# Memory norm's products spread on DVE, and four final products given to POOL and ACT, in a decoder layer on eight cores

## The chip, the cores and the metric

The kernel runs on one Trainium2 chip, on all 8 cores. Each core computes one of the eight batch entries, with no exchange between cores. The metric is the device time in microseconds of the slowest core, as the median of several runs. A profile is one execution, read on the slowest of its cores.

## The reference, cut to what matters

The layer is a SwiGLU half, a mixer of three branches (latent attention, gated linear attention, cross-attention into 256 memory tokens), a second SwiGLU half, and a final RMSNorm. The change touches the norm of the memory tokens and the final norm.

```python
def _rmsnorm(x, g):
    y = x * lax.rsqrt(jnp.mean(x * x, axis=-1, keepdims=True) + EPS)
    return y * g

def _swiglu(x, wg, wu, wd):
    return (jax.nn.silu(x @ wg) * (x @ wu)) @ wd

def _cross(xq, mem_n, w_kv):
    kv = (mem_n @ w_kv).reshape(B, M, 2, X_HEADS, X_DH)
    ...

h = x + 0.5 * _swiglu(_rmsnorm(x, ffn1_norm), ffn1_wg, ffn1_wu, ffn1_wd)
h = h + _mixer(h, mem, positions, ...)    # holds _cross(xq, _rmsnorm(mem, mem_norm), x_w_kv)
h = h + 0.5 * _swiglu(_rmsnorm(h, ffn2_norm), ffn2_wg, ffn2_wu, ffn2_wd)
return _rmsnorm(h, final_norm)
```

D_MODEL is 1024, D_FF 2816, and each core has 2048 tokens.

## The kernel before

**Tiles.** Activations lie with channels on the 128 partitions and tokens along the free axis. A core's 2048 tokens are four tiles of 512. The residual of a tile is eight slices of 128x512 in f32; three tiles' residuals are on the chip at once. Two of them are printed as `hS` in the rows, the third as `ntm`, because it shares that memory.

**The first channel mixer** (`ffn` with `f1_d`, the SwiGLU half) runs for tiles 0, 1 and 2 together. The 22 blocks of D_FF are cut into stages of 5, 5, 4, 4 and 4 (`SPLIT`, L443). A stage first does gate and up for each block and each of the tiles: 16 matmuls, a Silu on ACT, a product on DVE. Then it does the down products: for each of eight output slices and each tile one PSUM bank of 5 or 4 matmuls, and an evacuation on DVE, which adds it to the residual (`stt`, L599). The gate and up weights of a block are one DMA (`ring<-f1g`), the down weights of a stage of five are four DMAs (`ring<-f1d`, one for two of the eight slices); POOL's queue issues both, and they are converted from f32 to bf16 on the way. Seven ring buffers hold them (limit `rf`). POOL also issues `wb<-wm` conversions, which prepare later weights in DRAM.

**Memory keys and values** (`memory_kv`, L923) run inside the first mixer. At block 5 the memory tokens are loaded and normed: squares on ACT, a sum by matmuls with ones on PE, Ln and Exp on ACT for the reciprocal root, then eight products on DVE (`rmsnorm`, L751; `mb<-ma,vecs_s`, 128x256 each). At block 8 four weights `xw` are asked for, and 64 matmuls of 256 columns make keys and values.

**The ending** (`ending`, L1412) treats the last tile in two halves of 256 tokens. For each half come eight down products, their evacuations (128x256), squares on ACT and a sum in PSUM. Then per half `power` (L747) takes Ln and Exp, and eight products `scaled` (L811) multiply the residual slice by the final weight and the reciprocal root, in place. After the fourth and the eighth of them a DMA stores four slices.

**What sets the order.** Nothing is ordered by hand. Each operation is added with an engine and a cost, and `schedule` (L216) plays the program with these costs and writes down the order in which each engine takes them; on the chip each engine follows that order strictly. Among operations that are ready, the one with the lowest priority number goes first. The number is the operation's place in the program plus `f.base`, so a large `f.base` means: only when nothing nearer is ready. Pools of buffers are dealt in program order, ring buffers and PSUM banks by the planner. The waits are put in as semaphores, and `dma` (L205) passes through the same planner.

```python
op.pri = self.base + seq
...
pri = [op.pri for op in ops]
```

Of the kernel before, what the change touches and what calls it, by code (L numbers as in the profile page):

```python
# [13 lines left out]
D = 1024  # L14
# [443 lines left out]
def build_program():  # L458
# [185 lines left out]
    def vcol(c):  # L644
        return vecs[:, c:c + 1]
# [277 lines left out]
    def memory_kv():  # L923
        memf = [M2.get() for _ in range(4)]
        for i in range(4):
            f.dma("sp", memf[i], mem_d[i], nbytes=262144, after=f.last_pe, slack=12.0)
        src = [memf[c // 2][:, (c % 2) * 256:(c % 2 + 1) * 256] for c in range(8)]
        mt = [M1.get() for _ in range(4)]
        dst = [mt[c // 2][:, (c % 2) * 256:(c % 2 + 1) * 256] for c in range(8)]
        rmsnorm(src, [vcol(V_MEM + c) for c in range(8)], D, dst, NMEM, "n")  # L930
        M2.put(*memf)
        yield
        for half in range(2):
            wk = wload(xw_d[half], 8)
            for h2 in range(2):
                p = bank("n")
                mm([(p[:, 0:NMEM], wk[:, k, h2 * 128:(h2 + 1) * 128], dst[k], k == 0, k == 7) for k in range(8)])
                cp(kxT[:, half * 2 + h2, :], p[:, 0:NMEM])
        for half in range(2):
            wv = wload(xw_d[2 + half], 8)  # L940
            for mc in range(2):
                p = bank("n")
                mm([(p[:, 0:256], dst[k][:, mc * 128:(mc + 1) * 128], wv[:, k, :], k == 0, k == 7) for k in range(8)])
                cp(vx[:, mc, half * 256:(half + 1) * 256], p[:, 0:256])
        M1.put(*mt)
# [466 lines left out]
    def ending(i, w, act):  # L1412

        hh = [[T(hAP[i][:, c, h * 256:(h + 1) * 256], f"hh{h}_{c}") for c in range(8)] for h in range(2)]
        for h in range(2):
            for c in range(8):
                take_over([hh[h][c]], [hslot[i][c]])
        ps_ = []
        early = M2.get()
        actf(early[:, 0:1], eps_c, AF.Ln, extra_ins=(act[len(w[0]) - 1],))  # L1420
        M2.put(early)
        for h in range(2):
            cols = slice(h * 256, (h + 1) * 256)
            p = bank("n")
            ps_.append(p)
            for c in range(8):
                py = bank("f")
                m = len(w[c])
                for js in (range(m - 1), (m - 1,)) if h == 0 else (range(m),):
                    mm([(py[:, cols], w[c][j], act[j][:, cols], j == 0, j == m - 1) for j in js])  # L1430
                stt(hh[h][c], py[:, cols], 0.5, hh[h][c], ALU.mult, ALU.add)
                sq = M1.get()
                actf(sq[:, 0:256], hh[h][c], AF.Square, scale=D ** -0.5)
                mm([(p[:, 0:256], ones, sq[:, 0:256], c == 0, c == 7)])
                M1.put(sq)
        for h in range(2):
            r = M2.get()
            power(r[:, 0:256], ps_[h][:, 0:256], -0.5, EPS)
            for c in range(8):
                scaled(hh[h][c], hh[h][c], V_FIN, c, r[:, 0:256])  # L1440
                if c % 4 == 3:
                    op = f.dma("sp", out_d[3].rearrange("p (c n) -> p c n", c=8)[:, c - 3:c + 1, h * 256:(h + 1) * 256],
                               R(hh[h][c], hAP[i][:, c - 3:c + 1, h * 256:(h + 1) * 256]), ins=hh[h][c - 3:c], nbytes=524288)
                    outputs.add(op.seq)
# [126 lines left out]
```

How the kernel before makes its waits and increments, by code:

```python
    def emit(self, outputs, places, limits):  # L362
# [16 lines left out]
        def wait(e, evs):  # L379
            need = {}
            for (s, v), snap in evs:
                if known[e].get(s, 0) < v and need.get(s, (0, None))[0] < v:
                    need[s] = (v, snap)
            for s, (v, snap) in sorted(need.items(), key=lambda kv: -len(kv[1][1])):
                if known[e].get(s, 0) >= v:
                    continue
                self.handles[e].wait_ge(sems[s], v)
                k = known[e]
                k[s] = max(k.get(s, 0), v)
                for s2, v2 in snap.items():
                    if k.get(s2, 0) < v2:
                        k[s2] = v2
# [8 lines left out]
                        continue  # L401
                evs.append((p.ev, p.snap))
            fn = next(f for (x, f, _) in op.alts if x == e)
            if op.dma:
                nm = slots[e][turn[e] % len(slots[e])]
                turn[e] += 1
                if nm in last:
                    evs.append((last[nm].ev, last[nm].snap))
                wait(e, evs)
                counts[nm] += 16
                fn(self.handles[e]).then_inc(sems[nm], 16)
                op.ev = (nm, counts[nm])
                last[nm] = op
                if op.seq in outputs:
                    final.append(op)
            else:
                wait(e, evs)
                counts[e] += 1
                fn(self.handles[e]).then_inc(sems[e], 1)
                op.ev = (e, counts[e])
            op.snap = dict(known[e])
```

## Time and profile before

| | us |
|---|---|
| median of 3 runs | 1629.36 |
| lowest of them | 1628.25 |
| profiled execution, device time | 1627.07 |
| its slowest core (core 2), first to last instruction | 1626.0 |
| its other cores | 1618.5 to 1623.1 |

The sum in the prediction is made against the profiled execution: 1626.0 us of span and 1.07 around it. That execution is 2.29 under the median. In the rows, a time is measured from the start of the core's span, `x8` is a count, and the bracket at a row's end is the engine's idle time before it and what ended it. Engine names are PE (TensorE), PEld (its weight loads), DVE, ACT, POOL and SP.

### The profile page before, as it was taken

The numbers are of one execution on the slowest core, as the hardware profiler recorded it, in microseconds if no ns is written. First come the engines' busy times: TensorE is split into PE (matmuls) and PEld (weight loads), VectorE is DVE, ScalarE is ACT, GpSimd is POOL, SyncE is SP. The second block draws the span as 40 slices with busy tenths as digits, with TensorE's granted clock in tenths as the row PEclk, the third lists the DMA queues.
The fourth block names the chain that finished last, engine by engine and source line by source line (L and its number), as shares of the span: only waits on it lengthen the run. The fifth ranks groups of instructions, "written<-read, shape, count | busy, mean of one in ns | idle before, by whom it ended". The sixth has DMA issues, their size and how long they took to land.

```text
span 1626.0 us, 23823 instructions; the slowest of 8 cores (1618.5 to 1626.0 us)
## 1 busy us (share of the span) xinstructions
PE 1588.4 (98%) x7517; PEld 737.7 (45%) x7667; DVE 884.8 (54%) x1524; ACT 738.6 (45%) x1193; POOL 120.9 (7%) x227
## 2 busy tenths in 40 slices
PE   6999999999999999999999999999999999999997
PEld 2444444444444444444444444444444444444444
DVE  6666333557766466664565454476444445533347
ACT  5212211046765237882276874258587632311114
POOL 1101111100000000000000000000000000001000
PEclk9999999999999999999999999999999999999999
DMA  8779999997767455586787788587334344522212
GB/s 209 115 113 130 133 127 143 123 180 187 166 108 179 153 162 147 99 199 198 237 227 165 180 204 220 184 278 232 104 96 125 115 158 160 177 85 91 78 52 104
DMA packets 80712, 249.65 MB, mean 154 GB/s; under 512 B 9488, under 2 KB 13840, under 8 KB 80144
## 3 DMA queue, kind: packets, MB, share of 16 engines
q0 software_dynamic: 28720, 107.43, 38.3%
q1 hardware_dynamic: 51872, 140.70, 26.9%
q8 instruction: 66, 1.08, 0.3%
q14 instruction: 54, 0.44, 0.1%
HBM read 283.16 MB, written 54.26 MB: 208 GB/s over the span
## 4 chain that ended last, share of the span: by engine, by line
PE 94%; DMA 2%; DVE 1%; issue 1%; ACT 1%; POOL 0%; SPq 0%; DVEq 0%; ACTq 0%; POOLq 0%
PE ps_all L561 94%; DMA ring<-f1g 1%; DMA ring<-wb 1%; DVE hS L599 1%; DMA hS<-x 0%; ACT L587 0%; DVE mb L599 0%; ACT mb L587 0%; ACT ma L587 0%; DVE ntm L599 0%; PE ps_all L572 0%; DVE ma L594 0%; ACT fa L587 0%; DVE mb L611 0%; POOL ring L206 0%
## 5 line engine op out<-in xcount | busy, mean ns | idle before, releaser
L561 PE MATMUL ps_all<-ntm,ring 128*128 128x512 bf16 x2181 | 529.1, 379 | 3.6 <-ACT mb L587 0.6
L561 PE MATMUL ps_all<-B,ring 128*128 128x512 bf16 x1971 | 448.4, 379 | 2.7 <-DVE mb L594 0.2
L561 PEld LDWEIGHTS ps_all<-ntm,ring 128*128 128x128 bf16 x2224 | 217.1, 98 | 257.2 <-issue 4.3
L561 PEld LDWEIGHTS ps_all<-B,ring 128*128 128x128 bf16 x2016 | 196.6, 98 | 233.1 <-issue 1.1
L561 PE MATMUL ps_all<-aF,ring 128*128 128x512 bf16 (+1 forms) x1240 | 294.8, 374 | 4.9 <-DVE mb L599 3.1
L587 ACT ACTIVATE fa<-ps_all 128x512 f32<-128x512 f32 x170 | 101.3, 597 | 364.1 <-PE ps_all L561 351.8
L599 DVE SCALAR_TENSOR_TENSOR hS<-ps_all,hS 128x512 f32<-128x512 f32 (+1 forms) x256 | 170.1, 672 | 86.5 <-PE ps_all L561 85.4
L594 DVE TENSOR_TENSOR aF<-fa,ps_all 128x512 bf16<-128x512 f32 x151 | 103.2, 686 | 196.3 <-PE ps_all L561 186.1
L587 ACT ACTIVATE mb<-ps_all 128x512 bf16<-128x512 f32 (+1 forms) x304 | 165.5, 572 | 72.7 <-PE ps_all L561 70.6
L561 PEld LDWEIGHTS ps_all<-aF,ring 128*128 128x128 bf16 x1264 | 123.4, 98 | 143.6 <-issue 6.7
L587 ACT ACTIVATE ma<-ps_all,hv 128x512 f32<-128x512 f32 x104 | 71.1, 686 | 173.0 <-PE ps_all L561 164.9
L587 ACT ACT_TABLE_LOAD x91 | 116.8, 1283 | 71.9 <-PE ps_all L561 59.7
L599 DVE SCALAR_TENSOR_TENSOR ma<-ma,ps_all 128x512 f32<-128x512 f32 x96 | 65.7, 687 | 110.9 <-PE ps_all L561 105.5
L561 PE MATMUL ps_all<-mb,va 128*128 128x512 bf16 (+3 forms) x314 | 107.6, 347 | 0.4 <-DVE mb L594 0.3
L561 PE MATMUL ps_all<-mb,B 128*128 128x512 bf16 (+3 forms) x317 | 93.3, 347 | 0.9 <-ACT mb L587 0.4
L561 PE MATMUL ps_all<-mb,ring 128*128 128x512 bf16 (+1 forms) x407 | 92.9, 371 | 0.5
L599 DVE SCALAR_TENSOR_TENSOR fa<-fa,ps_all 128x512 f32<-128x512 f32 x66 | 45.1, 685 | 65.5 <-ACT fa L587 59.7
L587 ACT ACTIVATE ma<-ma 128x512 f32<-128x512 f32 (+2 forms) x121 | 73.2, 619 | 6.9 <-DVE ma L605 2.7
L587 ACT ACTIVATE ma<-ps_all 64x512 f32<-64x512 f32 (+2 forms) x96 | 57.1, 598 | 20.8 <-PE ps_all L561 17.9
L561 PEld LDWEIGHTS ps_all<-mb,ring 128*128 128x128 bf16 x416 | 40.6, 98 | 45.1 <-issue 0.5
L594 DVE TENSOR_TENSOR mb<-ma 128x512 bf16<-128x512 f32 (+1 forms) x60 | 41.3, 689 | 12.3 <-ACT ma L587 8.9
L206 POOL DMA_DIRECT2D ring<-f2bg x44 | 23.4, 531 | 320.0 <-PE ps_all L561 314.7
(139 smaller groups left out, 1193.8 us busy)
## 6 DMA issues: line engine op xcount, KB each, us to landing
ring<-wb SPq DMA_DIRECT2D x112, 512.0 KB, 4.7
ring<-f1g POOLq DMA_DIRECT2D x44, 512.0 KB, 8.5
ring<-f2bg POOLq DMA_DIRECT2D x44, 512.0 KB, 3.9
wb<-wm POOLq DMA_DIRECT2D x28, 512.0 KB, 13.8
ma<-spill SPq DMA_DIRECT2D x48, 256.0 KB, 4.8
ring<-wb SPq DMA_DIRECT2D x48, 256.0 KB, 3.8
ring<-f2g POOLq DMA_DIRECT2D x22, 512.0 KB, 7.8
f2bg<-ring SPq DMA_DIRECT2D x22, 512.0 KB, 6.9
```

What stands on the lines that cost most here:

```text
L206: op = self.add([(q, lambda e: e.dma_start(out=_ap(out), in_=_ap(in_)), 0.9 if q == "pool" else 0.06)], outs=[out, *outs], ins=[in_, *ins] ...
L561: i = e.matmul(_ap(o), lhsT=_ap(l), rhs=_ap(r), start=st, stop=sp)
L587: f.add([("act", lambda e: e.activation(out=_ap(out), in_=_ap(in_), func=func, scale=_ap(scale), **kw), c_act(out, bias is not None))], ou ...
L594: f.add([(eng, lambda e: e.tensor_tensor(out=_ap(out), in0=_ap(a), in1=_ap(b), op=op), c_dve(out, rate))], outs=[out], ins=[a, b, *extra_ins])
L599: f.add([("dve", lambda e: e.scalar_tensor_tensor(out=_ap(out), in0=_ap(in0), scalar=_ap(scalar), in1=_ap(in1), op0=op0, op1=op1), c_dve(o ...
```

## The change

The eight products of the memory norm are no longer added through `rmsnorm`. They are added one by one with `f.base = LATER // 2`, a declared cost of 1.2 us, and the same operands and operation. In the ending, slices 2 and 6 of each half are no longer one DVE instruction: POOL multiplies the slice by the reciprocal root (declared cost 0.8 us), and ACT multiplies the result by the final weight with a Copy.

```diff
-        rmsnorm(src, [vcol(V_MEM + c) for c in range(8)], D, dst, NMEM, "n")
-        M2.put(*memf)
+        p = mean_square(src, D, NMEM, "n", M2, M1)
+        rstd = M2.get()
+        power(rstd[:, 0:NMEM], p[:, 0:NMEM], -0.5, EPS)
+        f.base = LATER // 2
+        for c in range(8):
+            f.add([("dve", lambda e, c=c: e.scalar_tensor_tensor(
+                out=_ap(dst[c]), in0=_ap(src[c]), scalar=_ap(vcol(V_MEM + c)), in1=_ap(rstd[:, 0:NMEM]),
+                op0=ALU.mult, op1=ALU.mult), 1.2)], outs=[dst[c]], ins=[src[c], vcol(V_MEM + c), rstd])
+        f.base = 0
+        M2.put(rstd, *memf)
...
-                scaled(hh[h][c], hh[h][c], V_FIN, c, r[:, 0:256])
+                if c in (2, 6):
+                    f.add([("pool", lambda e, o=hh[h][c], r=r[:, 0:256]: e.tensor_tensor(
+                        out=_ap(o), in0=_ap(o), in1=_ap(r), op=ALU.mult), 0.8)], outs=[hh[h][c]], ins=[hh[h][c], r])
+                    actf(hh[h][c], hh[h][c], AF.Copy, scale=vcol(V_FIN + c))
+                else:
+                    scaled(hh[h][c], hh[h][c], V_FIN, c, r[:, 0:256])
```

**DVE, the down products of the second stage.** `ntm` and `hS` rows are evacuations, `mb<-ma,vecs_s` rows are the memory norm's products. Before:

```order
L599 SCALAR_TENSOR_TENSOR hS<-ps_all,hS 128x512 x2
L599 SCALAR_TENSOR_TENSOR mb<-ma,vecs_s 128x256 x8
L599 SCALAR_TENSOR_TENSOR ntm<-ps_all,ntm 128x512
L599 SCALAR_TENSOR_TENSOR hS<-ps_all,hS 128x512 x2
L599 SCALAR_TENSOR_TENSOR ntm<-ps_all,ntm 128x512
L599 SCALAR_TENSOR_TENSOR hS<-ps_all,hS 128x512 x2
```

After:

```order
L599 SCALAR_TENSOR_TENSOR hS<-ps_all,hS 128x512 x2
L599 SCALAR_TENSOR_TENSOR ntm<-ps_all,ntm 128x512
L935 SCALAR_TENSOR_TENSOR mb<-ma,vecs_s 128x256 x2
L599 SCALAR_TENSOR_TENSOR hS<-ps_all,hS 128x512 x2
L935 SCALAR_TENSOR_TENSOR mb<-ma,vecs_s 128x256
L599 SCALAR_TENSOR_TENSOR ntm<-ps_all,ntm 128x512
L599 SCALAR_TENSOR_TENSOR hS<-ps_all,hS 128x512
L935 SCALAR_TENSOR_TENSOR mb<-ma,vecs_s 128x256
L599 SCALAR_TENSOR_TENSOR hS<-ps_all,hS 128x512
L599 SCALAR_TENSOR_TENSOR ntm<-ps_all,ntm 128x512
L599 SCALAR_TENSOR_TENSOR hS<-ps_all,hS 128x512
L935 SCALAR_TENSOR_TENSOR mb<-ma,vecs_s 128x256
```

The block of eight is broken up: two stand together, then four stand singly between evacuations, and the last two come after the stage's last evacuation.

**PE, the same stage.** `aF` and `ntm` rows are down products, `mb,ring` and `ring,mb` are the 64 matmuls of the memory's keys and values, `B,ring` are gate and up products of the next stage. Before:

```order
L561 MATMUL ps_all<-aF,ring 128x512 x4
L561 MATMUL ps_all<-mb,ring 128x256 x32
L561 MATMUL ps_all<-ring,mb 128x256 x32
L561 MATMUL ps_all<-aF,ring 128x512 x2
L561 MATMUL ps_all<-ntm,ring 128x512 x4
L561 MATMUL ps_all<-aF,ring 128x512 x4
L561 MATMUL ps_all<-ntm,ring 128x512
```

After:

```order
L561 MATMUL ps_all<-aF,ring 128x512 x5
L561 MATMUL ps_all<-ntm,ring 128x512
L561 MATMUL ps_all<-aF,ring 128x512
L561 MATMUL ps_all<-B,ring 128x512 x20
L561 MATMUL ps_all<-mb,ring 128x256 x32
L561 MATMUL ps_all<-ring,mb 128x256 x32
L561 MATMUL ps_all<-B,ring 128x512 x168
L561 MATMUL ps_all<-aF,ring 128x512 x3
```

Before, the 64 stand inside the down products, and 41 down matmuls follow them before the first `B,ring`. Now all down products come first, then 20 gate and up matmuls, then the 64.

**ACT, the end of the program.** `mb<-hS` are squares, `ma<-ps_all,eps_c` is a half's Ln, `ma<-ma` its Exp, `hS<-hS,vecs_s` the new Copies. Before:

```order
L587 ACTIVATE ma<-ps_all,eps_c 128x256
L587 ACTIVATE mb<-hS 128x256
L587 ACTIVATE ma<-ma 128x256
L587 ACTIVATE mb<-hS 128x256 x2
L587 ACTIVATE ma<-ps_all,eps_c 128x256
L587 ACTIVATE ma<-ma 128x256
```

After:

```order
L587 ACTIVATE ma<-ps_all,eps_c 128x256
L587 ACTIVATE mb<-hS 128x256
L587 ACTIVATE ma<-ma 128x256
L587 ACTIVATE mb<-hS 128x256 x2
L587 ACTIVATE hS<-hS,vecs_s 128x256
L587 ACTIVATE ma<-ps_all,eps_c 128x256
L587 ACTIVATE hS<-hS,vecs_s 128x256
L587 ACTIVATE ma<-ma 128x256
L587 ACTIVATE hS<-hS,vecs_s 128x256 x2
```

One Copy now stands in front of the second half's Ln and one between that Ln and its Exp. POOL's four products are the last four instructions of its own queue, and DVE has 12 products where it had 16.

## Rows read from the trace of the kernel before

**Rows 1.** The page: busy time by engine, and the chain that ended last, by engine.
```profile
PE 1588.4 (98%) x7517; PEld 737.7 (45%) x7667; DVE 884.8 (54%) x1524; ACT 738.6 (45%) x1193; POOL 120.9 (7%) x227
...
PE 94%; DMA 2%; DVE 1%; issue 1%; ACT 1%; POOL 0%; SPq 0%; DVEq 0%; ACTq 0%; POOLq 0%
```

**Rows 2.** Spans and granted clock of the cores.
```profile
core 2: 1626.0 us, clock 0.997
...
core 5: 1622.8 us, clock 0.998
...
core 7: 1623.1 us, clock 0.998
```

**Rows 3.** Waits of PE, 150 to 200 us, core 2, then core 0: total, times, longest.
```profile
PE ps_all L561 <- DVE mb L599: 3.1, 1, 3.1
...
PE ps_all L561 <- DMA ring<-f1d: 0.9, 1, 0.9
```

**Rows 4.** Timeline of core 2 around 166 us: start, length, engine, line, operation.
```profile
165.73 0.69 DVE L599 SCALAR_TENSOR_TENSOR hS<-ps_all,hS 128x512 f32<-128x512 f32 x1 [0.87 <-PE ps_all L561]
166.34 3.25 DVE L599 SCALAR_TENSOR_TENSOR mb<-ma,vecs_s 128x256 bf16<-128x256 f32 x8
...
168.94 1.12 PE L561 MATMUL ps_all<-aF,ring 128*128 128x512 bf16 x4 [3.10 <-DVE mb L599]
...
174.51 3.66 PE L561 MATMUL ps_all<-mb,ring 128*128 128x256 bf16 x32
...
178.00 3.66 PE L561 MATMUL ps_all<-ring,mb 128*128 128x256 bf16 x32
```

**Rows 5.** POOL's issue of the third down weights, core 2, and its landing.
```profile
L206 POOL DMA_DIRECT2D ring<-f1d x1: 557/557/557, 153.8 to 153.8; - x1
DMA to landing us min/median/max: 14.9/14.9/14.9
```

**Rows 6.** Core 1, the same stretch: timeline row, then busy time and clock.
```profile
163.80 3.25 DVE L599 SCALAR_TENSOR_TENSOR mb<-ma,vecs_s 128x256 bf16<-128x256 f32 x8
...
163.00:168.00 5.00, 4.89 (x27) 2.35 (x26) 4.81 (x11) 0.12 (x1) 0.56 (x1) 1.00 1.35 157
```

**Rows 7.** Core 2: busy time in 5 us; PE, PEld, DVE, ACT, POOL, clock, DMA.
```profile
170.00:175.00 5.00, 4.78 (x19) 2.06 (x19) 1.57 (x3) 0.00 (x0) 0.00 (x0) 0.68 0.90 114
```

**Rows 8.** POOL's issue of the next gate weights, and landing: core 2, then core 5.
```profile
L206 POOL DMA_DIRECT2D ring<-f1g x1: 562/562/562, 166.5 to 166.5; - x1
DMA to landing us min/median/max: 16.4/16.4/16.4
...
L206 POOL DMA_DIRECT2D ring<-f1g x1: 562/562/562, 167.0 to 167.0; - x1
DMA to landing us min/median/max: 16.0/16.0/16.0
```

**Rows 9.** First matmuls on those gate weights: core 2, then core 5.
```profile
190.35 1.03 PE L561 MATMUL ps_all<-B,ring 128*128 128x512 bf16 x4
...
187.96 1.03 PE L561 MATMUL ps_all<-B,ring 128*128 128x512 bf16 x4
```

**Rows 10.** Timeline of the end of core 2.
```profile
1615.84 0.40 ACT L587 ACTIVATE ma<-ma 128x256 f32<-128x256 f32 x1
...
1616.16 0.96 ACT L587 ACTIVATE mb<-hS 128x256 bf16<-128x256 f32 x2
1616.53 6.41 DVE L599 SCALAR_TENSOR_TENSOR hS<-hS,vecs_s,ma 128x256 f32<-128x256 f32 x16
...
1617.63 0.47 ACT L587 ACTIVATE ma<-ps_all,eps_c 128x256 f32<-128x256 f32 x1 [0.51 <-PE ps_all L561]
1618.20 0.42 ACT L587 ACTIVATE ma<-ma 128x256 f32<-128x256 f32 x1
```

**Rows 11.** DVE's nearest rows: products of two SBUF tiles, and the scan.
```profile
L594 DVE TENSOR_TENSOR ma<-ma,mb x2: 425/425/425, 61.8 to 62.9; 128x256 f32<-128x256 f32 x2
...
L1019 DVE TENSOR_TENSOR_SCAN ma<-smask_s,ma 128x512 f32<-128x512 bf16 x8 | 9.6, 1218 | 11.0 <-ACT ma L587 11.0
```

## Prediction

> **What bounds the kernel.** I read the page first. PE is busy for 98% of the span, and 94% of the chain that ended last is PE [rows 1]. So an edit on DVE pays only where PE waits, or at the very end, where PE has nothing left. The cores differ by some us, and the slowest counts [rows 2]. Next come the waits of PE. Around 166 us core 2 has one of 3.1 us, which the profile puts down to DVE's `mb`, the memory norm's products [rows 3]. It is just what the first part of the change is aimed at, so I looked at that place in the timeline: DVE is in the eight products from 166.34 to 169.59, PE starts again at 168.94 [rows 4]. But PE starts before the block has ended, and what it runs are down products, which read no `mb`. Then I looked at POOL's issues. The down weights that this very matmul reads left POOL's queue at 153.8 and landed 14.9 us later, at 168.7; PE starts 0.2 later [rows 5]. Core 0 waits at the same place, and there the profile names these weights [rows 3]. Core 1, a few us earlier in its program, has the same block of eight on DVE from 163.80 to 167.05, and PE is busy 4.89 of 5.00 us over it [rows 6]. So the wait is the transfer's. The eight products fill a pause that PE has anyway, and where it has none the PSUM banks cover them.
>
> **Part 1, what it removes.** Nothing at that place: the down weights are issued as before. If the wait were DVE's after all, 3.1 us would go, and with it the low clock that follows. From 170 to 175 us the granted clock is a mean of 0.68 [rows 7], between the levels of 1.2 and 2.4 GHz, just after the pause, and costs (1 - 0.68) x 5 = 1.6 us. The products cost DVE the same wherever they stand, 3.25 / 8 = 0.41 us each [rows 4]; an evacuation is 0.69 [rows 4], and PE fills a bank of five in about 1.1, so one of each just fits, and the spare banks take the rest.
>
> **Part 1, what it moves.** This is the part that I give weight. On PE the 64 memory matmuls, 2 x 3.49 = 6.98 us by their start times [rows 4], stood ahead of the first gate matmuls of the next stage. Now they stand behind 20 of these, so those matmuls want their weights 6.98 us earlier. The order of POOL's queue up to that DMA is unchanged, so it is issued and lands when it did. Core 2: issued at 166.5, landing at 182.9 [rows 8]; wanted at 190.35 - 6.98 = 183.4 [rows 9], so no wait, by half a us, and only because the earlier pause had delayed PE. Core 5: issued at 167.0, landing at 183.0 [rows 8]; wanted at 187.96 - 6.98 = 180.98 [rows 9]. That is a new wait of 2.0 us. I take the others, which paused little there or not at all like core 1 [rows 6], to be of core 5's kind. The later loads are asked for by PE's progress and have more room: the next block's weights take the buffer of the third down weights, which are now done before the 64 matmuls and not after. I expect no second wait there.
>
> For the slowest core: on the profiled figures core 5 rises from 1622.8 to 1624.8 [rows 2], core 2 stays at 1626.0, and nothing changes. But the pause that makes core 2 last is the luck of one transfer; in another execution the slowest may be a core like 5, at +2.0. I take the middle, +1.0, with 0 and +2.0 as ends.
>
> **Part 2, the tail.** The first reciprocal root is ready at 1615.84 + 0.40 = 1616.24. DVE's 16 products run from 1616.53 to 1622.94, 6.41 / 16 = 0.40 each, with no gap, and the second root, ready at 1618.62, is never waited for [rows 10]. Four of them go: 1.6 us at most. What takes their place is a chain: a POOL product of T, then a Copy on ACT, for which I take the 0.42 of the Exp on a tile of that size, with 0.1 from one instruction to the next (1618.10 to 1618.20 [rows 10]). ACT does its queue in order, and the Copy of slice 6 stands between the second half's Ln and its Exp. Hence the second root is ready at 1616.3 + 2T + 0.5 + 0.5 = 1617.3 + 2T, and the last slice at that + 2T + 0.5 = 1617.8 + 4T. DVE for its part ends at the later of 1616.53 + 6 x 0.40 and the root, + 2.4. For T = 0.425, DVE's own time for such a product [rows 11], that is 1621.3 and the full 1.6 is won. The chain passes the old end of 1622.94 at T = 1.28. No POOL arithmetic of this size is in the trace, so T is open. Below I put 0.425; above I put four times that, 1.7, which gives 1617.8 + 6.8 = 1624.6, or +1.7. I take T = 1.2, the nearest row of a slow vector instruction on SBUF tiles, DVE's scan at 1.218 [rows 11]: 1622.6, or -0.3. The last store follows the last product as before.
>
> The Trainium skill (GPSIMD Engine Reference, section Elementwise, side-by-side cycle accounting) gives about 2.6 cycles an element at 1.2 GHz for a product of two tensors on POOL. By it T would be an estimated 0.55 us plus dispatch, and the tail would win its full 1.6 us if nothing else were in the way; no run here shows it yet.
>
> **Sum.** Part 1 +1.0, tail -0.3: +0.7 on the profiled execution, 1627.07 to 1627.8. Against the median, 2.29 higher, 1629.36 + 0.7 = 1630.1. A measurement of this kernel can tell about 2%, some 33 us, from no change, so this is no change.
>
> **Rivals.**
> 1. POOL and DVE run freely beside each other and T is at most 0.9. Speaks for it that T may be twice DVE's 0.425 [rows 11] and the chain still ends in time; against it that DVE works without a gap on the same tiles all the while. The tail gives -1.6, part 1 +1.0: 1628.8.
> 2. POOL's and DVE's products exclude each other. Both kinds read two SBUF tiles. Place: the last 7 us. With T = 0.8 the shared time is 12 x 0.40 + 4 x 0.8 = 8.0 us against 6.41, +1.6. If DVE, being back to back, always goes first, POOL's first pair starts only after DVE's six (2.4 later), and so does its second: 1617.8 + 3.2 + 4.8 = 1625.8, +2.9. Mean +2.2, with part 1 +3.2: 1632.6. It decides as soon as the last POOL product ends after 1622.4. For it: ACT's order makes every delay of POOL a delay of the second root. Against: the trace has no POOL arithmetic to show a collision. The Trainium skill (SBUF, State Buffer, section Who interferes with whom) says that a DVE instruction with two SBUF inputs contends with a GpSimd instruction that reads SBUF, and that the one which comes second is blocked fully. By that rule this rival holds; no row here bears on it.
> 3. The wait at 166 us is DVE's, as the profile names it. Then 3.1 + 1.6 goes, and with the tail's -0.3 the time is 1629.36 - 5.0 = 1624.4. Against it stands the landing at 168.7.
> 4. The new wait is followed by a low clock, as the old one was on core 2: +2.0 + 1.6 - 0.3 = +3.3, 1632.7. Against it: it took 3.1 us there.
>
> **How the numbers follow.** Forecast 0.34, rival 1 0.25, rival 2 0.27, rival 3 0.06, rival 4 0.08. The predicted time is the forecast's, 1630.1. The range holds all but rival 3: down to 1626.5, which is rival 1 with part 1 at 0 (1627.8) less the 1.1 by which the lowest run lies under the median; up to 1634.5, the worse of rivals 2 and 4 with 1.5 for spread and for T above 0.8. No case comes near 33 us. I leave 0.01 for faster and 0.02 for slower, which only an unforeseen cost could bring: the first use of an arithmetic instruction on POOL, or a transfer stage that falls behind.
>
> **What would show it.** Right: the pause before the third down weights is still there on cores late in their program, with eight products no longer beside it; most cores other than the last show a wait of PE of 1 to 2 us ahead of the first gate matmuls of the third stage, ended by the landing of `ring<-f1g`; DVE's 12 final products have a gap between the sixth and the seventh, ended by ACT. Wrong, if the wait at 166 us is gone on every core with that landing as late as before (rival 3); if DVE's six products take longer than 0.40 each or POOL's wait for their end (rival 2); if POOL's products take under 0.9 us and the last store starts 1.6 us earlier after the last matmul (rival 1); if a clock under 1.00 follows the new wait (rival 4).

## The result, and the profile after

| | before | after |
|---|---|---|
| median, us (9 runs each) | 1628.41 | 1634.37 |
| profiled execution, device time, us | 1627.07 | 1632.85 |
| its slowest core, us | 1626.0 | 1631.8 |
| mean of its eight cores, us | 1621.3 | 1628.9 |

The ratio is 1.0048, with a 95% interval of 1.0036 to 1.0060: the change makes the kernel slower by about 8 us (0.0048 x 1628). That is far under 2%, but clear of zero. Some executions, three of the nine of before among them, were disturbed: they ran at a lower clock and took up to 2000 us, and all ratios here leave them out, while the medians of the table, which differ by 6.0 us, hold them. I forecast +0.7 us.

The page of after. These rows answer to [rows 1], and the third is the row of the gate and up matmuls with the idle time before them.

```profile
PE 1598.2 (98%) x7667; PEld 736.3 (45%) x7667; DVE 884.9 (54%) x1520; ACT 740.2 (45%) x1197; POOL 124.3 (8%) x231
...
PE 92%; DMA 4%; DVE 1%; ACT 1%; issue 1%; POOL 0%; SPq 0%; DVEq 0%; ACTq 0%; POOLq 0%
...
L561 PE MATMUL ps_all<-B,ring 128*128 128x512 bf16 x2016 | 453.2, 380 | 4.2 <-DMA ring<-f1g 4.0
```

DMA has gone from 2% to 4% of the chain that ended last, and `ring<-f1g` now holds up these matmuls for 4.0 us on this core. DVE's busy time has not moved (884.8 to 884.9), though it has four instructions fewer.

It is not one unlucky core: all eight are longer, by 4.0 (core 7) to 11.6 us (core 4, 1618.5 before and 1630.1 now) or 11.7 (core 1). So the rows to read are of the cores that had no wait before. PE's waits of after from 170 to 400 us, on cores 0, 4 and 6 (each: total, times, longest):

```profile
PE ps_all L561 <- DMA ring<-f1g: 6.3, 2, 4.5
...
PE ps_all L561 <- DMA ring<-f1g: 4.8, 2, 3.3
PE ps_all L561 <- ACT mb L587: 2.3, 1, 2.3
...
PE ps_all L561 <- DMA ring<-f1g: 6.8, 2, 5.0
```

In before none of these three has a wait there of that size. Their places on core 4:

```profile
178.77 4.48 PE L561 MATMUL ps_all<-B,ring 128*128 128x512 bf16 x20 [1.45 <-DMA ring<-f1g]
183.08 3.66 PE L561 MATMUL ps_all<-mb,ring 128*128 128x256 bf16 x32
186.57 3.66 PE L561 MATMUL ps_all<-ring,mb 128*128 128x256 bf16 x32
...
323.90 3.61 PE L561 MATMUL ps_all<-B,ring 128*128 128x512 bf16 x16 [3.31 <-DMA ring<-f1g]
...
369.54 0.38 PE L561 MATMUL ps_all<-mb,ones 128*128 128x512 bf16 x1 [2.31 <-ACT mb L587]
```

The first, 1.45 us, is the one that I forecast: the 20 gate matmuls now come ahead of the 64. The second (3.31) comes 145 us later, in the last stage of the mixer, and the third (2.31) 190 us later, at the sum of a norm; neither was forecast. The other even cores have the second one larger (5.0 on core 6), the odd ones have smaller ones or the third alone. The third is put down to ACT, but ACT had waited for a store, `rstd<-ma`, that was issued at 342.5 and landed at 364.1 (before: 337.1 and 355.5). ACT's row:

```profile
364.27 1.28 ACT L587 ACT_TABLE_LOAD   x1 [4.55 <-DMA rstd<-ma]
```

From there it goes over ACT's Ln, Exp and squares to PE's sum at 369.54. So both later waits start with a DMA that lands late (core 3 is the same: 5.1 us of ACT's idle time end with that store). (Where no row is shown, here and below, a wait is given as the spacing of two matmul starts, with 0.2 us of work in it.) And most of the large ones have a low clock beside or behind them: on core 0, behind the wait that ends at 325.1, and on core 4, behind its third,

```profile
324.00:328.00 4.00, 2.94 (x8) 1.13 (x9) 0.00 (x0) 0.00 (x0) 0.00 (x0) 0.65 1.11 182
370.00:374.00 4.00, 4.00 (x12) 1.47 (x11) 3.67 (x6) 2.47 (x5) 0.00 (x0) 0.57 1.02 348
```

the columns being busy time of PE, PEld, DVE, ACT and POOL, then the granted clock: 0.65 after core 0's wait, 0.57 after core 4's third. The level in such a stretch is the lower of the two, 1.2 GHz; a mean of 0.57 over 4 us is 3.4 us at half speed. Core 4's account up to 469 us: waits 1.45 + 3.31 + 2.31 = 7.1 and a low clock of 3.4 us at half speed, 1.7, make 8.8 of the 9.5 us by which the same matmul starts later (469.2, now 478.7).

**Where the transfers stand.** The timeline of POOL's queue on core 4, before, with the landing of all loads from 170 to 200 us (min/median/max) as its last row:

```profile
175.49 1.02 POOL L206 DMA_DIRECT2D wb<-wm  x2 [2.95 <-PE ps_all L561]
176.50 0.55 POOL L206 DMA_DIRECT2D ring<-f1g  x1
177.04 0.75 POOL L206 DMA_DIRECT2D ring<-f1d  x1
179.04 0.72 POOL L206 DMA_DIRECT2D ring<-f1d  x1 [1.25 <-PE ps_all L561]
...
DMA to landing us min/median/max: 11.7/16.3/23.9
```

The same of after:

```profile
185.53 0.53 POOL L206 DMA_DIRECT2D ring<-f1g  x1 [7.15 <-PE ps_all L561]
187.30 0.72 POOL L206 DMA_DIRECT2D ring<-f1d  x1 [1.24 <-PE ps_all L561]
190.76 1.03 POOL L206 DMA_DIRECT2D wb<-wm  x2 [2.73 <-PE ps_all L561]
197.71 0.97 POOL L206 DMA_DIRECT2D wb<-wm  x2 [5.93 <-PE ps_all L561]
...
DMA to landing us min/median/max: 5.9/9.5/18.3
```

Before, five loads leave between 175.5 and 179.8 us, and the queue is full: a load takes up to 23.9 us to land. After, the gate load that stood at 176.50 leaves at 185.53 and lands after only 5.9 us: the queue was nearly empty. What POOL waits for is PE, because a load needs a ring buffer that PE has finished with. And here is the thing that I had overlooked: the four weights `xw` of the memory sit in four of the seven ring buffers until the 64 matmuls have read them, and these now end at 190.2 instead of 175.0 on this core (186.57 + 3.66 above; 171.31 + 3.66 in the second row of before here, under the row of the `xw` loads, first and last issue):

```profile
L206 POOL DMA_DIRECT2D ring<-xw x4: 527/528/530, 86.7 to 109.1; - x4
...
171.31 3.66 PE L561 MATMUL ps_all<-ring,mb 128*128 128x256 bf16 x32
```

With them held, POOL had nothing to fill. There is a second tie. The two conversions `wb<-wm` that stand at 175.49 and now at 190.76 need no ring buffer; they are asked for right after the 64 in the program, with `after=f.last_pe` (L636), so they wait for the last of the 64, and leave 0.5 us behind it in both kernels. No run here separates the two ties.

The DMA engines' share and rate (the last two columns) over 64 us say what that costs, before and then after, and then the 120 us that follow, before and after:

```profile
176.00:240.00 64.00, 63.68 (x293) 28.98 (x297) 24.73 (x36) 8.45 (x13) 10.10 (x18) 1.00 1.06 137
...
176.00:240.00 64.00, 62.55 (x323) 31.30 (x321) 20.36 (x31) 11.52 (x21) 11.09 (x20) 1.00 0.97 124
...
200.00:320.00 120.00, 119.42 (x547) 54.41 (x556) 49.00 (x71) 13.73 (x23) 18.58 (x35) 1.00 1.01 130
...
200.00:320.00 120.00, 120.00 (x557) 54.41 (x556) 48.91 (x71) 13.31 (x23) 18.41 (x34) 1.00 1.01 120
```

13 GB/s less over 64 us are 0.83 MB, an estimated 6.9 us at the 120 GB/s at which the stream goes on in after. On each of the eight cores the share is lower over this stretch than before, 0.94 to 0.99 in after and 0.99 to 1.06 in before; the mean rate is 123.6 and 132.5 GB/s, which makes an estimated 4.6 us. From 200 to 320 us core 4's share stands at 1.01 in both: the stream fills the engines, so what was not moved by then was not made up before the conversions ended. (The rate in this stretch is lower too, 120 GB/s against 130, at the same share. I can't explain that, so the bytes give the debt only roughly.) The last gate weights of the first channel mixer show the debt come due. On core 4 they left POOL at 290.2 before and at 292.1 after:

```profile
L206 POOL DMA_DIRECT2D ring<-f1g x1: 558/558/558, 290.2 to 290.2; - x1
...
L206 POOL DMA_DIRECT2D ring<-f1g x1: 558/558/558, 292.1 to 292.1; - x1
```

and landed at 316.8 and 323.7. PE restarts at 323.90. Issued 1.9 later, landed 6.8 later.

**The end of the program.** The timeline of after, core 2, against [rows 10]:

```profile
1621.36 1.58 POOL L1449 TENSOR_TENSOR hS<-hS,ma 128x256 f32<-128x256 f32 x2 [49.54 <-ACT ma L587]
1621.49 6.62 DVE L599 SCALAR_TENSOR_TENSOR hS<-hS,vecs_s,ma 128x256 f32<-128x256 f32 x12
...
1623.45 0.40 ACT L587 ACTIVATE ma<-ma 128x256 f32<-128x256 f32 x1
1623.70 4.92 SPq L206 DMA_DIRECT2D outT<-hS  x4
1623.99 1.86 POOL L1449 TENSOR_TENSOR hS<-hS,ma 128x256 f32<-128x256 f32 x2 [1.05 <-ACT ma L587]
...
1625.95 0.51 ACT L587 ACTIVATE hS<-hS,vecs_s 128x256 f32<-128x256 f32 x1 [0.35 <-POOL hS L1449]
```

Twelve products now take 6.62 us, where sixteen took 6.41. It is not a wait for ACT: the second root is ready at 1623.85, and DVE has no gap between the sixth and the seventh. The rows of single products, DVE and then POOL, show what it is:

```profile
1621.49 0.86 DVE L599 SCALAR_TENSOR_TENSOR hS<-hS,vecs_s,ma 128x256 f32<-128x256 f32 x1
...
1623.14 0.47 DVE L599 SCALAR_TENSOR_TENSOR hS<-hS,vecs_s,ma 128x256 f32<-128x256 f32 x1
...
1625.19 0.94 DVE L599 SCALAR_TENSOR_TENSOR hS<-hS,vecs_s,ma 128x256 f32<-128x256 f32 x1
...
1621.36 0.71 POOL L1449 TENSOR_TENSOR hS<-hS,ma 128x256 f32<-128x256 f32 x1 [49.54 <-ACT ma L587]
```

A DVE product with a POOL product beside it lasts 0.86 to 0.94 us from issue to end, one without 0.47 (0.40 from start to start). The starts of the twelve are 0.79, 0.86, 0.40, 0.40, 0.40, 0.86, 0.86 and then 0.40 apart: four of them lose 0.39 to 0.46 each, as many as POOL has products. From the first product to the end of the span it is 10.3 to 10.4 us on every core of after, where it was 9.5.

### The profile page after: what moved, and what is told of

Read it like the earlier page. It is cut to its first block, busy times and chain, and to the rows that moved or that the text cites. A ratio compares the mean times of both kernels' runs of the same rounds, so it can differ in the third digit from the quotient of the medians.

```text
span 1631.8 us, 23988 instructions; the slowest of 8 cores (1627.1 to 1631.8 us)
## 1 busy us (share of the span) xinstructions
PE 1598.2 (98%) x7667; PEld 736.3 (45%) x7667; DVE 884.9 (54%) x1520; ACT 740.2 (45%) x1197; POOL 124.3 (8%) x231
## 4 chain that ended last, share of the span: by engine, by line
PE 92%; DMA 4%; DVE 1%; ACT 1%; issue 1%; POOL 0%; SPq 0%; DVEq 0%; ACTq 0%; POOLq 0%
PE ps_all L561 92%; DMA ring<-f1g 2%; DMA ring<-f1d 1%; DVE hS L599 1%; ACT L587 1%; DMA hS<-x 0%; DMA ring<-wb 0%; ACT mb L587 0%; ACT ma L587 0%; DVE ntm L599 0%; POOL wb L206 0%; PE ps_all L572 0%; DVE aF L594 0%; ACT fa L587 0%; DVE mb L611 0%
## 5 line engine op out<-in xcount | busy, mean ns | idle before, releaser
L561 PE MATMUL ps_all<-B,ring 128*128 128x512 bf16 x2016 | 453.2, 380 | 4.2 <-DMA ring<-f1g 4.0
L561 PE MATMUL ps_all<-mb,va 128*128 128x512 bf16 (+1 forms) x320 | 110.0, 348 | 0.3 <-DVE mb L594 0.3
L561 PE MATMUL ps_all<-mb,B 128*128 128x512 bf16 (+1 forms) x320 | 94.3, 347 | 0.5 <-ACT mb L587 0.4
```

Of the source, the lines that this page charges most:

```text
L561: i = e.matmul(_ap(o), lhsT=_ap(l), rhs=_ap(r), start=st, stop=sp)
```

## The experiments

Each kernel ran five rounds beside the kernel before on the same chip; ratios are to before. "First part" is the edit on the memory norm, "second part" that on the ending.

**1 and 2. Each part alone.** The diff is the first, then the second hunk of the change.

```diff
-        rmsnorm(src, [vcol(V_MEM + c) for c in range(8)], D, dst, NMEM, "n")
+        p = mean_square(src, D, NMEM, "n", M2, M1)
...
```

> Only the memory norm's part of the change; the ending is that of before. Theory L (the loads are late: the 64 memory matmuls moved behind the stage's down products, and with them the order of POOL's loads): nearly the whole loss is here, +4 to +7 us on the kernel before (ratio 1.003 to 1.004), with PE waits for gate weights of 1 to 3 us near 180 us and of 3 to 5 us near 325 us on most cores. Theory T (the tail is the larger part, the waits in the first mixer are an accident of the executions): +0 to +2 us.

Measured: 1.0046 (1.0034 to 1.0058). Waits of 1.6 to 3.1 us near 182 on six cores, then 3.2 to 5.8 near 330 on three, 2.4 to 6.5 near 370 on four others, with a low clock beside most; three of those near 182 have one too.

```diff
-                scaled(hh[h][c], hh[h][c], V_FIN, c, r[:, 0:256])
+                if c in (2, 6):
...
```

> Only the ending's part of the change; the first mixer is that of before. Theory L: no new wait before the end; the tail from the first final product on DVE to the end of the span is 0.8 to 0.9 us longer than before (about 10.3 against 9.5 us), the whole +0.5 to +1 us. Theory T: +4 us or more, with a longer tail than that. A theory in which POOL helps: the tail is shorter by up to 1.6 us.

Measured: 1.0006 (0.9996 to 1.0016); 10.3 to 10.6 us from the first final product to the end of the span, against 9.5. That is +0.8 us or a little more, under what five rounds resolve, but seen in the traces of all 16 cores that have this ending. The loss of the change is the first part's.

**3. The products in one block, the 64 matmuls late.** DVE's eight products stand together again, and PE's and POOL's rows are those of after; a DMA that nobody needs and that the planner takes for slow pushes the 64 back.

```diff
+        late = f.dma("sp", dly, ident_d, after=len(f.ops) - 1, nbytes=65536, slack=5.0)
...
+                f.ops[-1].deps.add(late.seq)
                 cp(kxT[:, half * 2 + h2, :], p[:, 0:NMEM])
```

> The eight products in one block on DVE as before, but the planner is made to believe that the 64 memory matmuls become ready later (they also depend on a small transfer that it takes to be slow), so that PE's order is that of the changed kernel row by row and POOL's too. Theory L: as slow as the memory part alone, +4 to +7 us, with the waits near 180 and 325 us. Theory P (products between the evacuations hold up the evacuations, and this is what costs): back at the time of before, within 2 us, no wait near 180 or 325 us.

Measured: 1.0046 (1.0033 to 1.0059), with waits of 2.1 to 3.1 near 182 on six cores, of 5.0 to 5.6 near 330 on three, and of 1.9 to 3.5 near 370 on five. It is the first part's time without its spreading. So the cost lies in where the 64 matmuls stand, and not in what DVE does.

**4. The products spread, the 64 matmuls nearly where they were.** The first part with a declared cost of 0.4 instead of 1.2 us: five products stand together and three singly, the 64 move by only 9 down matmuls, POOL's order is that of before.

```diff
-                op0=ALU.mult, op1=ALU.mult), 1.2)], outs=[dst[c]], ins=[src[c], vcol(V_MEM + c), rstd])
+                op0=ALU.mult, op1=ALU.mult), 0.4)], outs=[dst[c]], ins=[src[c], vcol(V_MEM + c), rstd])
```

> The products with the low priority of the changed kernel but their true cost of 0.4 us declared: three of the eight stand singly between evacuations, five together, the 64 memory matmuls move behind 9 down matmuls only, and POOL's order is row by row that of before. Theory L: the time of before within 2 us, no wait for gate weights near 180 us, the wait for the third down weights near 168 us still there on cores late in their program. Theory P: half or more of the loss of the memory part, +2 to +4 us.

Measured: 1.0011 (0.9998 to 1.0024). No wait near 182 or 325; the one near 170 is still there on all cores (0.7 to 4.2 us), so the block of eight was not its cause, and three cores wait 2.7 to 4.2 near 366. The mirror image of the run before: spread, and nearly free.

**5, 6 and 8. Fewer conversions where the stream is full.** The conversions `wb<-wm` are three a block from block 14 to 17 and two otherwise. In 5 (after) and 6 (before) the third ones move to blocks 18 to 21, in 8 (before) four go to the merge of the first tile.

```diff
-        for _ in range(3 if 14 <= j < 18 else 2 if j >= 3 else 0):
+        for _ in range(3 if j >= 18 else 2 if j >= 3 else 0):
```

> The changed kernel, with one conversion fewer per block in the fourth stage of the first mixer (two a block instead of three, blocks 14 to 17) and one more per block in the last stage (blocks 18 to 21). Memory matmuls and loads up to the fourth stage stay as in the changed kernel. Theory L (the transfers fall some 6 us behind after 186 us and are late for the last gate weights near 325 us): with four conversions, about 12 us of transfer, out of the way, the waits near 325 and 370 us are gone and the one near 180 us stays; 3 to 6 us of the loss come back, ratio to the kernel before 1.000 to 1.002. A rival (the wait near 325 us is set by something else that the memory part moved): the waits stay, ratio 1.004 or more.

> The same shift of four conversions in the kernel before. Theory L: that kernel has only small waits near 320 to 370 us in some executions (none to 2 us), so it gains 0 to 2 us, ratio 0.998 to 1.000. A rival (the later conversions are wanted at once by the mixer of tile 0): new waits for weights at 430 to 530 us, ratio over 1.002.

> The kernel before with two conversions a block throughout the first mixer and the last four (the output projection's) issued at the head of tile 0's merge. Theory L: no wait for weights between 300 and 380 us, gain 0 to 2 us, ratio 0.998 to 1.000, unless the merge waits for its weights.

Measured: 1.0105 (1.0085 to 1.0125), 1.0071 (1.0058 to 1.0084) and 1.0138 (1.0119 to 1.0156). The wait near 325 is gone in 5 and 6, but one of 4.3 to 7.3 us stands near 375, in 5 and 6 alike, and run 8 waits for the deferred conversions themselves. The rows are of 5 (170 to 400 us), then of 8 (500 to 560 us):

```profile
PE ps_all L561 <- DMA ring<-wb: 6.5, 1, 6.5
...
PE ps_all L561 <- DMA ring<-wb: 12.2, 1, 12.2
```

Theory L's times (1.000 to 1.002 for 5, 0.998 to 1.000 for 6 and 8) did not come, and the waits of 5 and 6 stand where neither theory had them; for 8 a wait at the merge had been allowed for. The three don't tell the theories apart. Moving a conversion changes what the planner writes for the whole rest of the program, so too many things differ. What was wanted was a kernel with the same order and fewer bytes.

**9, 10 and 12. The same order, fewer bytes.** In the kernel of the first part alone (9, 12) and in before (10), conversions carry a quarter of their columns: from the thirteenth on in 9 and 10, only the fourteenth and fifteenth in 12. The planner is told the old size, so that every engine's order is the same; later stages read an earlier conversion's data instead, and their loads no longer wait for their own conversion. (The thirteenth is asked for at block 9, the fifth of the second stage, and not at the fourth, as the expectation has it.)

```diff
-        f.dma("pool", wb_T[i][:, 0:n], wm_d[i][:, 0:n], nbytes=128 * n * 4, after=f.last_pe)
+        m = n // 4 if i >= 12 else n
+        f.dma("pool", wb_T[i][:, 0:m], wm_d[i][:, 0:m], nbytes=128 * n * 4, after=f.last_pe)
...
-        f.dma("sp", t[:, 0:n], wb_T[b][:, 0:n], nbytes=128 * n * 2)
+        f.dma("sp", t[:, 0:n], R(wb_T[b], wb_d[b if b < 12 else 10][:, 0:n]), ins=[wb_T[10]], nbytes=128 * n * 2)
```

> The kernel of the first part alone, in which every conversion wb<-wm from the thirteenth on (asked for from the fourth block of the second stage) carries only a quarter of its columns; later stages read an earlier conversion's data in their place, so the output is another. Order, number of instructions and waits stay. Theory A (the 64 matmuls' later place costs POOL's stream of transfers about 6 us, the stream is full until the mixer's end, so PE meets the debt near 325 or 370): no wait of PE over 1 us and no low clock between 200 and 400 us, the wait of 1 to 3 us near 182 stays because its weights are asked for earlier; time within 3 us of before (ratio 0.998 to 1.002). Theory B (the late weights are late because their buffers come free late, whatever the stream carries): waits of 3 us or more near 325 or 370 stay, ratio 1.0045.

Measured: 0.9974 (0.9963 to 0.9986). No core has a wait over 0.6 us from 190 to 460 us, nor a low clock there; near 182 three cores wait 1.4, 1.5 and 2.6 us.

> The same thin conversions in the kernel before: the control. Both theories: the waits at 164 to 170 us stay, nothing else changes in the mixer, ratio 0.998 to 1.000; the difference between this and the first part with thin conversions is then the price of the wait near 182 alone, 1 to 3 us.

Measured: 0.9960 (0.9947 to 0.9973). The control was wrong in one point: the waits near 164 to 170 are gone too, all but pauses of 0.6 us, since the first thin conversions stand in POOL's queue ahead of them. Hence 0.4% is what before itself pays for the fullness of the stream. Between 9 and 10 it is 0.0014 of 1628 us, 2.3 us, for the wait near 182; the two intervals overlap, so this is a rough figure. With the full stream the first part costs 0.46%, with the thin one 0.14%: the rest, about 5 us, it costs only where the stream is full.

> The kernel of the first part alone, with only the fourteenth and fifteenth conversions cut to a quarter of their columns (786 of 1049 KB of bf16 not written, about 6 us at the 126 GB/s that the stream carries here). Theory A, with a debt of about 6 us: that pays it, the waits near 325 and 370 are all or nearly all gone (under 1 us), ratio near 1.001. If the debt is larger, or comes from something else than bytes, waits of over 2 us and the low clock stay on several cores, ratio above 1.003.

Measured: 0.9980 (0.9970 to 0.9989). The share of the DMA engines, core 1, first part alone, then with two thin conversions, then with all:

```profile
240.00:320.00 80.00, 80.00 (x373) 36.30 (x371) 37.48 (x55) 7.76 (x13) 10.46 (x19) 1.00 0.98 122
...
240.00:320.00 80.00, 80.00 (x372) 36.25 (x371) 34.79 (x51) 8.36 (x14) 12.58 (x23) 1.00 1.01 127
...
240.00:320.00 80.00, 80.00 (x372) 36.31 (x371) 33.24 (x49) 8.96 (x15) 12.40 (x23) 1.00 0.48 74
```

Two transfers shortened by an estimated 6 us in all, with every instruction in its place, take away 0.66% of the time (1.0046 to 0.9980): the largest waits near 330 and 370 are 1.4 and 2.6 us, no clock falls, and the total is under that of before, which has such waits in some executions as well (2.1 us near 322 and 2.2 to 4.2 near 366 on four cores of run 11, whose mixer is that of before). That is theory A, though waits of over 1 us were not expected and the gain is larger than forecast. With theory B, late buffers alone, nothing would have changed. But 0.66% is 10.8 us, more than the first part costs, and not all of it is the later waits: one of the two thin conversions stands ahead of the third down weights (issued at 154.9 on core 4, the other at 201.6), so the waits of up to 4.1 us near 170 are gone as well, and before has those too. There is no before with the same two thin conversions; the pair 9 and 10 is the cleaner evidence. In 9 the share falls to 0.48, the stream is no longer full, and the late buffers near 190 us cost nothing later.

But for the tail, before, after and these kernels differ in the first 435 us only. DVE's first scan, as a mean of the eight cores of the profiled execution, starts at 422.6 us in before, 428.7 in after, 432.0 in run 1, 431.6 in 3, 426.5 in 4, 422.8 in 9, 422.0 in 10 and 423.3 in 12; from there to the end it is 1198.6 to 1200.5 us in all of them. So the bytes and the waits that are missing behind the mixer in 9, 10 and 12 don't bear on the comparison.

**7. The reciprocal root in PSUM for DVE.** The second part, with the root for DVE's twelve products left in PSUM, and a second Exp that writes it to SBUF for POOL.

```diff
-            power(r[:, 0:256], ps_[h][:, 0:256], -0.5, EPS)
+            actf(ps_[h][:, 0:256], ps_[h][:, 0:256], AF.Ln, bias=eps_c)
+            actf(r[:, 0:256], ps_[h][:, 0:256], AF.Exp, scale=-0.5)
+            actf(ps_[h][:, 0:256], ps_[h][:, 0:256], AF.Exp, scale=-0.5)
...
-                    scaled(hh[h][c], hh[h][c], V_FIN, c, r[:, 0:256])
+                    scaled(hh[h][c], hh[h][c], V_FIN, c, ps_[h][:, 0:256])
```

> The ending's part of the change alone, but the reciprocal root lies in PSUM for DVE's twelve products and in SBUF, by a second Exp on ACT, for POOL's four: a DVE product then has one SBUF operand and not two. Theory S (DVE's and POOL's products of two SBUF tiles exclude each other, which is why twelve take 6.6 us and not 4.8): DVE's twelve come back to 0.40 to 0.42 us each while POOL works, the tail is shorter than that of the ending's part alone by 0.5 to 1.5 us. A rival (DVE waits for the second root, which ACT's Copies delay): twelve products still span 6 us or more with a gap of over 1 us between the sixth and the seventh, each at 0.40.

Measured: 1.0008 (0.9992 to 1.0023). Groups of the end of core 1 (busy time, mean ns of one, idle before), the second part alone, then this kernel:

```profile
L599 DVE SCALAR_TENSOR_TENSOR hS<-hS,vecs_s,ma 128x256 f32<-128x256 f32 x12 | 6.6, 622 | 0.0
...
L1441 POOL TENSOR_TENSOR hS<-hS,ma 128x256 f32<-128x256 f32 x4 | 3.5, 878 | 50.3 <-ACT ma L587 50.3
...
L599 DVE SCALAR_TENSOR_TENSOR hS<-hS,vecs_s,ps_all 128x256 f32<-128x256 f32 x12 | 5.3, 477 | 1.5 <-ACT ps_all L587 0.9
...
L1443 POOL TENSOR_TENSOR hS<-hS,ma 128x256 f32<-128x256 f32 x4 | 2.8, 719 | 50.5 <-ACT ma L587 50.5
```

A POOL product falls from a mean of 878 to 719 ns, a DVE product from 622 to 477. POOL's first pair is nearly over when DVE starts, but its second runs beside DVE, and there POOL's products take 0.72 and DVE's follow each other at 0.39 to 0.40. The collision is of two SBUF operands: take one of them away on DVE's side and both engines gain. But the sequence of products has gaps now (5.3 of 5.95 us are busy), DVE starts 1.0 later for the extra Exp, and the tail, counted from that later start, is still 10.1 to 10.3 us. From the last matmul's start to the end it is 10.4 to 10.5 us, against 9.6 to 9.9 with the collision and 8.7 to 8.8 in before. The end did not become shorter, as had been expected.

**11. Four products left out.** Slices 2 and 6 of each half are not multiplied at all.

```diff
-                scaled(hh[h][c], hh[h][c], V_FIN, c, r[:, 0:256])
+                if c not in (2, 6):
+                    scaled(hh[h][c], hh[h][c], V_FIN, c, r[:, 0:256])
```

> The kernel before with four of the last tile's sixteen final products (slices 2 and 6 of each half) left out altogether, so these slices of the output are not multiplied: what POOL and ACT could give at most if they cost nothing. If DVE's products set the end, the time from the first product to the end of the span falls from 9.5 us by 1.6, less a gap of some tenths. If the four stores of 512 KB, 1.5 us each at the 350 GB/s of the end, set it, it falls by 0.4 to 0.6 only, the first store starting 0.4 us earlier.

Measured: 0.9999 (0.9987 to 1.0010). The twelve products take 4.83 us, as a product of 0.40 us says. But the tail is only 8.9 to 9.0 us long, 0.5 less than before. The last four stores, before and then this kernel (landing min/median/max, and the row of their issues, this kernel with its products):

```profile
DMA to landing us min/median/max: 3.0/3.0/3.1
1618.27 5.12 SPq L206 DMA_DIRECT2D outT<-hS  x4
...
DMA to landing us min/median/max: 3.0/3.5/4.0
1619.24 4.83 DVE L599 SCALAR_TENSOR_TENSOR hS<-hS,vecs_s,ma 128x256 f32<-128x256 f32 x12
...
1620.58 3.93 SPq L206 DMA_DIRECT2D outT<-hS  x4
```

From the first store's issue to the end of the fourth's it is 3.93 us instead of 5.12, but the slowest lands after 4.0 instead of 3.1. The rate by slices of 0.75 us in this kernel,

```profile
GB/s 399 229 0 0 0 0 0 0 0 0 0 0 0 0 0 217 324 355 332 346 333 348 348 194 0 0 0 0 0 0 0 0 0 0 0 0 0 0 0 0
```

stands near 340 from the first store on. Four times 512 KB (2.10 MB) at that rate are an estimated 6.2 us; the last landed 7.6 us behind the first store's issue. With 1.6 us of products gone, the stores have become what the end waits for.

**13 and 14. The same relief with all work kept.** Four conversions leave blocks 14 to 17 of before and are asked for at the head of the first tile's projections (13) or attention (14).

```diff
-        for _ in range(3 if 14 <= j < 18 else 2 if j >= 3 else 0):
+        for _ in range(2 if j >= 3 else 0):
...
         f.mark(f"proj{t}")
+        for _ in range(4 if t == 0 else 0): convert(todo.pop(0))
```

> The kernel before with four conversions (the mixer's output weights) taken out of the saturated blocks 14 to 17 of the first channel mixer and asked for at the head of the first tile's projections, all work kept. If the bytes of the mixer's stream are what PE pays for, its waits near 320 to 370 us are absent; whether the time falls hangs on what four conversions cost there: at the share of 0.70 to 0.74 that the DMA engines show from 380 to 500 us they should cost nothing, ratio 0.997 to 1.000. If the planner's new order puts another stage out of step, as in the two runs that moved conversions before, a wait of over 5 us appears after 400 us and the ratio is above 1.004.

> As the run above, but the four conversions are asked for at the head of the first tile's attention part, later. The same two outcomes; the wait of 10 to 13 us that these conversions brought at the head of the merge should not be there, since their readers come some tens of us later.

Measured: 1.0405 (1.0388 to 1.0422) and 1.0125 (1.0102 to 1.0148). The waits of 320 to 370 us are gone in both, as expected. But, in 13 and then in 14:

```profile
PE ps_all L561 <- DMA ring<-wb: 27.1, 6, 24.5
...
PE ps_all L561 <- DMA ring<-wb: 6.9, 2, 5.7
```

one wait of 24.5 us near 650 for a reader of the deferred weights, and some two dozen more of 0.5 to 6 us in 13, a dozen or so in 14, from the planner's new order. The relief is real and was given back several times over. No version that keeps all the work and beats before came out of this.

## Why the prediction was wrong

The time rose, as forecast, and 1634.37 lies in the range of 1626.5 to 1634.5, but only just: it rose by 8 us where I had +0.7.

1. *"So the wait is the transfer's."* Right. Spread over the evacuations (run 4, and after), the eight products leave the wait near 169 where it was; thinner transfers ahead of it (run 10) take it away. The trap goes on in after: the wait of 2.3 us near 179 on core 3 is put down to the products on line 935, which these matmuls don't read; the gate weights landed at 178.7 and PE restarts at 178.89.
2. *"That is a new wait of 2.0 us."* Right in place and size: spacings of 1.4 to 2.7 us near 180 on all cores but core 2, for which I said none. Runs 9 and 10 price it at some 2.3 us, with intervals that overlap. The +1.0 that I took, the middle between 0 and +2.0, is likely less than half of it.
3. *"The later loads are asked for by PE's progress and have more room [...] I expect no second wait there."* **This is the step that failed.** It put the cost of all later loads at nothing. It followed one buffer, that of the third down weights, and not the four that the `xw` weights hold until the 64 matmuls have read them, nor the two conversions that wait for the last of the 64. POOL's gate load moved from 176.5 to 185.5, those conversions from 175.5 to 190.8, the queue ran nearly dry, and a stream that is otherwise full until the mixer's end ran 5 to 7 us late. That came back 140 to 190 us further on as waits of 3 to 5 us on five of the eight cores, and each of the five has a stretch of low clock. Run 3 shows that the place of the 64 does it, and runs 9 and 10 that it costs about 5 us only where the stream is full; run 12 points the same way.
4. The low clock (rival 4) did come, but behind the waits that I had not foreseen, and in after never behind the first (in run 1 behind it on three cores, in run 3 on two): one stretch of 3.4 us at half speed, 1.7 us, as the 1.6 of [rows 7] had it; on core 6 it lasts 6.8 us and begins while PE still waits. I had named "a transfer stage that falls behind" among the unforeseen costs without working it out.
5. The tail: -0.3 forecast, +0.8 found. **The term that was mis-sized is the one for DVE**, which I let run at 0.40 whatever POOL did, so that the end hung on ACT's chain alone. T itself is 0.79 and 0.93 us as means of the two pairs, under the 1.2 taken, so the chain over ACT ends at 1626.46 on core 2, before DVE does (1628.11). Undisturbed, in run 7, T is 0.70, above the 0.55 that I had estimated without dispatch. Rival 2 held in its mechanism, that the two engines' products hold each other up: 12 x 0.40 + 0.39 + 3 x 0.46 = 6.6 us, against 6.62 measured; what POOL takes off DVE it gives back in waiting. They don't exclude each other in full: one product of each takes 0.86 us together, where 0.40 + 0.70 would make 1.10. That is one reason why the rival's price (2.2 us) was too high.

   The Trainium skill's rule (SBUF, State Buffer, section Who interferes with whom) says that a DVE instruction with two SBUF inputs contends with a GpSimd instruction that reads SBUF. These rows and run 7 agree with that. That the one which comes second is blocked in full, the rows don't show: 0.86 is less than 1.10.

   The +0.8 on core 2 is made up of three terms. The last store is issued 6.75 us after the first product and not 6.49, since DVE's block is longer; it lands after 3.3 us and not 3.0 (it is issued 1.2 us behind the third and not 1.6, which may be why); and the last row of the span stands 0.2 behind the landing, where it stood under 0.1 behind it. The first store is issued 0.47 later (1623.70 - 1621.49 = 2.21 against 1618.27 - 1616.53 = 1.74), but it and the next two land after 3.0 to 3.1 us, as before, so that delay is not what the end pays for.
6. *"The full 1.6 is won"* for a fast POOL was wrong as well. Run 11 shows the most that there was to win by taking four products off DVE: 0.5 us, because the stores take over.
7. The sum by what was found: new wait 2.3 + later waits and their clock some 5 (7.5 for the first part by run 1, less 2.3) + tail 0.8 = 8.3, against 7.8 measured (0.0048 x 1628.4). The 5 is a remainder and not a measurement of its own, so the sum tests only that the two parts add up.

## What to carry to other kernels

When matmuls are moved later, list every buffer that they hold and everything that waits for the last of them, not only the buffer that the next load happens to take. If the queue behind them is a stream that runs full, as here from 200 to 320 us, loads that leave late are a debt that stays until the stream thins out, and it can fall due far from the edit. To test such a cause, keep the order and change the bytes: kernels that relieve a stream by moving work also get a new plan, and here all five of them were slower.

Work moved from DVE to POOL won nothing here, where both read two SBUF operands at the same time. And at the end of a program ask first what the last stores allow.

## What the runs showed of the hardware

- DVE's and POOL's products of 128x256 f32, each of two SBUF operands, hold each other up only while both are at work: a DVE product costs 0.40 us of its queue alone and 0.79 to 0.86 beside POOL. The POOL product costs 0.70 beside DVE products that read PSUM (1.40 for two), 0.79 and 0.93 beside ones that read SBUF.
- In the first channel mixer, where POOL's converting loads are most of the traffic, the DMA engines move 120 to 135 GB/s at a share of 1.0; plain stores reach 348 GB/s at the end of the program. The mean of 153 GB/s on the page of after hides that.
- A granted clock of 0.5 for 3.4 or 6.8 us goes with many of the longer waits, but not with all. Between 160 and 460 us, in the profiled executions of all kernels here, it stands at all 24 waits of over 4.3 us and at 24 of the 42 between 2.5 and 4.3 us (idle time by the spacing, the 0.2 us of work taken off), and it begins from 3.7 us before PE restarts to 1.3 us behind. In after, core 4's 3.31 us near 324 are followed by 1.00, its 2.31 near 369 by 0.57.
- Not explained: with the root in PSUM some DVE products follow each other at 0.39 us and others at 0.58; and which of the two later waits a core gets.
